# An expert's overflow products in two visits of TensorE, and their activations transposed by halves

## The reference

```python
logits = jnp.matmul(xt, w_router).astype(jnp.float32) + b_router.astype(jnp.float32)
top_logit, top_idx = lax.top_k(logits, TOP_K)            # TOP_K = 4, 32 experts
gates = jax.nn.softmax(top_logit, axis=-1)
...
gu = lax.ragged_dot(xs, w_gate_up, group_sizes) + b_gate_up[e_sorted]
gate, lin = jnp.split(gu, 2, axis=-1)
gate = jnp.minimum(gate, SWIGLU_LIMIT)                   # 7.0
lin = jnp.clip(lin, -SWIGLU_LIMIT, SWIGLU_LIMIT)
act = (lin + 1.0) * (gate * jax.nn.sigmoid(SWIGLU_ALPHA * gate))
out = lax.ragged_dot(act, w_down, group_sizes) + b_down[e_sorted]
```

## Time and profile before

| what | us |
|---|---|
| median of 3 runs | 2567.62 (2565.17 to 2568.31) |
| span of the profiled execution | 2566.9 |
| TensorE busy | 2471.5 (96%) |
| VectorE busy | 1506.3 (59%) |
| ScalarE busy | 1226.7 (48%) |
| GpSimd busy | 329.9 (13%) |

### The profile page before, as it was taken

How to read it: one execution, slowest core, us unless ns; L and a number is a source line. 1 busy time by engine, 2 the same in 40 slices (tenths; PEclk the granted TensorE clock), 3 DMA queues, 4 the chain that set the end, 5 groups by cost and what they waited for, 6 DMA issues and landing times.

```text
span 2566.9 us, 41888 instructions
## 1 busy us (share of the span) xinstructions
PE 2471.5 (96%) x14427; PEld 1980.3 (77%) x14428; DVE 1506.3 (59%) x1486; ACT 1226.7 (48%) x1246; POOL 329.9 (13%) x379
## 2 busy tenths in 40 slices
PE   8999999999999989976999999999999999999996
PEld 7987777998888878974788777777777886778775
DVE  4312333332333235355789876888876997688877
ACT  6413444220112021064577665666655775667665
POOL 0000000000000000042121212121121221212110
PEclk9999999999999999997999999999999999999998
DMA  4133243224332212447789987898977997899988
GB/s 129 34 50 54 66 73 80 49 50 49 50 50 81 99 66 91 146 167 263 257 317 384 371 296 257 319 381 287 369 252 258 376 381 271 306 335 331 387 278 304
DMA packets 262285, 536.68 MB, mean 209 GB/s; under 512 B 28952, under 2 KB 79896, under 8 KB 261120
## 3 DMA queue, kind: packets, MB, share of 16 engines
q1 hardware_dynamic: 241184, 488.96, 57.3%
q0 software_dynamic: 21024, 46.65, 6.7%
HBM read 492.92 MB, written 42.63 MB: 209 GB/s over the span
## 4 chain that ended last, share of the span: by engine, by line
PE 51%; DMA 1%; DVE 1%; issue 0%; ACT 0%; POOL 0%; ACTq 0%; POOLq 0%; DVEq 0%
PE m_y L2158 5%; PE m_gate L2158 5%; PE m_gate L2162 4%; PE m_lin L2158 4%; PE m_gate L2160 4%; PE m_lin L2162 4%; PE m_lin L2160 4%; PE m_y L2160 4%; PE m_y L2162 4%; PE m_spill L2200 4%; PE m_turn L2212 2%; PE m_turn L2150 1%; PE m_gate L2168 1%; PE m_y L2168 1%; PE m_spill L2196 1%; PE m_lin L2168 1%
## 5 line engine op out<-in xcount | busy, mean ns | idle before, releaser
L1973 DVE TENSOR_TENSOR m_w_lo<-raw,m_w_hi 128x2048 fp32r<-128x2048 f32 x384 | 874.6, 2288 | 253.7 <-ACT m_w_hi L1847 234.8
L1847 ACT CAST m_w_hi<-raw 128x2048 fp32r<-128x2048 f32 x384 | 733.3, 1911 | 446.2 <-PE m_lin L2162 230.1
L106 PE MATMUL c_bank<-h_hi_r,ring_hi 128*128 128x512 f32 x640 | 251.7, 393 | 0.9 <-PEq L396 0.9
L108 PE MATMUL c_bank<-h_lo_r,ring_hi 128*128 128x512 f32 x640 | 249.5, 390 | 0.0
L109 PE MATMUL c_bank<-h_hi_r,ring_raw_r 128*128 128x512 f32 x640 | 249.2, 389 | 0.0
L147 ACT CAST ring_hi<-ring_raw 128x2048 fp32r<-128x2048 f32 x43 | 82.1, 1908 | 280.4 <-DMA ring_raw<-in_w_in 128.3
L2158 PE MATMUL m_gate<-m_w_hi,m_x_hi 128*128 128x512 f32 x512 | 209.6, 409 | 0.0
L2158 PE MATMUL m_y<-m_w_hi,m_a_hi 128*128 128x512 f32 x512 | 206.1, 403 | 1.5 <-DVE m_a_lo L2025 1.5
L2162 PE MATMUL m_gate<-m_w_hi,m_x_lo 128*128 128x512 f32 x512 | 201.1, 393 | 0.0
L2160 PE MATMUL m_y<-m_w_lo,m_a_hi 128*128 128x512 f32 x512 | 201.0, 393 | 0.0
L2158 PE MATMUL m_lin<-m_w_hi,m_x_hi 128*128 128x512 f32 x512 | 200.7, 392 | 0.0
(11 more groups left out here) (336 smaller groups left out, 4539.9 us busy)
## 6 DMA issues: line engine op xcount, KB each, us to landing
raw<-in_w_gate_up SPq DMA_DIRECT2D x512, 512.0 KB
raw<-in_w_down SPq DMA_DIRECT2D x256, 512.0 KB, 12.3
ring_raw<-in_w_in SPq DMA_DIRECT2D x31, 1024.0 KB, 9.4
gates<-work POOLq DMA_DIRECT2D x32, 256.0 KB, 2.6
work<-gates SPq DMA_DIRECT2D x8, 1024.0 KB, 7.2
v<-in_x SPq DMA_DIRECT2D x8, 512.0 KB, 12.5
ring_raw<-in_w_branch_b SPq DMA_DIRECT2D x4, 1024.0 KB, 5.3
ring_raw<-in_w_branch_a SPq DMA_DIRECT2D x4, 1024.0 KB, 5.2
```

Of the source, the lines that this page charges most:

```text
L106: pe.matmul(out, left_hi(k), right_hi(k), start=first and k == kts[0], stop=False, skip_group_check=True)
L108: pe.matmul(out, left_hi(k), right_lo(k), start=False, stop=False, skip_group_check=True)
L1847: act.copy(w_hi[:, p % WS].rearrange("p k b n -> p (k b n)"), raw[:, raw_slot(m)].rearrange("p k b n -> p (k b n)")).then_inc(signals.whi, 1)
L1973: dve.tensor_tensor(w_lo[:, p % WS].rearrange("p k b n -> p (k b n)"), raw[:, raw_slot(m)].rearrange("p k b n -> p (k b n)"), f32(w_hi[:, ...
```

## The change

TensorE's overflow products move into two visits. Behind p 5 stand `s_down(8)`, `s_down(9)` and `s_gate_up(4)` to `(7)`; behind p 11 stand `s_down(10)`, `s_down(11)` and, for the next expert, `s_gate_up(0)` to `(3)`. Ahead of the loop all four `s_gate_up` stand behind panel 3. Since the down product of panels 8 and 9 needs only the first half of the activations, each half is transposed alone: `s_turn(0)` behind p 4, `s_turn(1)` ahead of the panel of p 10, both into `p_turn`, and copied by `as_copy` at steps 5 and 10. The sums share one bank now: `s_y` (down) and `s_h` (one half of gate and up at a time) are the two halves of `p_spill`, and the second half's bias matmul no longer sets `start`. `store` waits, with the overflow's rows, for the next expert's four gate-up products in that bank, and `pick_expert(0, ..)` moves from step 3 of VectorE to step 5.

```diff
+        s_y, s_h = p_spill[:, 0:256], p_spill[:, 256:512]
...
-            def as_copy(hb, nb):
+            def as_copy(j, hb, nb):
                 with act.If(hb > 0):
-                    act.wait_ge(signals.s_turned, nb + (OPEN + 1))
-                    act.copy(a_s[:, :, :].rearrange("p k c -> p (k c)"), p_gate[1][:, 0:256]).then_inc(signals.s_copied, 1)
+                    act.wait_ge(signals.s_turned, 2 * nb + (OPEN + j + 1))
+                    act.copy(a_s[:, 4 * j:4 * j + 4].rearrange("p k c -> p (k c)"), p_turn[:, 0:P]) \
+                        .then_inc(signals.s_copied, 1)
...
                     act.wait_ge(signals.s_dn, 4 * nb + (OPEN + 4))
-                    act.activation(ys_out[:, :], p_turn[:, 0:256], ACT.Copy,
+                    act.wait_ge(signals.s_gu, GU * nb + 4 * hb_next + (OPEN + GU))
+                    act.activation(ys_out[:, :], s_y, ACT.Copy,
...
+                    if p == 5:
+                        as_copy(0, hb, nb)
-                    if p == 9:
-                        as_copy(hb, nb)
+                    if p == 10:
+                        as_copy(1, hb, nb)
...
                     if p == 3 and not tail:
                         x_split(0, t + 1)
+                    if p == 5 and not tail:
                         dve.wait_ge(signals.panel_done, count(t, 0))
                         dve.wait_ge(signals.s_gu, GU * nb + 5 * hb + OPEN)
                         pick_expert(0, t + 1, signals.picked_gu)
...
-            def s_turn(nb):
-                pe.wait_ge(signals.s_activated, 2 * nb + (OPEN + 2))
-                for j in range(2):
-                    tr = pe.transpose(p_gate[1][:, j * P:(j + 1) * P], act_s[:, j], cst["ident"][:, :])
-                tr.then_inc(signals.s_turned, 1)
+            def s_turn(j, hb, nb):
+                with pe.If(hb > 0):
+                    pe.wait_ge(signals.s_activated, 2 * nb + (OPEN + j + 1))
+                    pe.transpose(p_turn[:, 0:P], act_s[:, j], cst["ident"][:, :]).then_inc(signals.s_turned, 1)
...
                     if p == 10:
                         pe.wait_ge(signals.alo, 2 * t + (OPEN + 2))
+                        s_turn(1, hb, nb)
...
-                    if 2 <= p <= 5:
+                    if p == 4:
+                        s_turn(0, hb, nb)
+                    if p == 5:
                         with pe.If(hb > 0):
-                            if p == 2:
-                                pe.wait_ge(signals.s_taken, 2 * nb + (OPEN + 1))
-                            s_gate_up(p + 2)
+                            pe.wait_ge(signals.s_copied, 2 * nb + (OPEN + 1))
+                            pe.wait_ge(signals.s_taken, 2 * nb + (OPEN + 1))
+                            pe.wait_ge(signals.s_stored, nb + OPEN)
+                            s_down(8)
+                            s_down(9)
+                            for panel in range(4, GU):
+                                s_gate_up(panel)
...
-                    if 8 <= p <= 11 and not tail:
-                        with pe.If(hb_next > 0):
-                            if p == 8:
-                                pe.wait_ge(signals.xs_copied, nb + hb + (OPEN + 1))
-                                pe.wait_ge(signals.s_taken, 2 * nb + 2 * hb + OPEN)
-                            s_gate_up(p - 8)
-                    if p == 10:
-                        with pe.If(hb > 0):
-                            pe.wait_ge(signals.s_copied, nb + (OPEN + 1))
-                            s_down(8)
-                            s_down(9)
                     if p == 11:
                         with pe.If(hb > 0):
+                            pe.wait_ge(signals.s_copied, 2 * nb + (OPEN + 2))
                             s_down(10)
                             s_down(11)
+                    if p == 11 and not tail:
+                        with pe.If(hb_next > 0):
+                            pe.wait_ge(signals.xs_copied, nb + hb + (OPEN + 1))
+                            pe.wait_ge(signals.s_taken, 2 * nb + 2 * hb + OPEN)
+                            pe.wait_ge(signals.s_stored, nb + OPEN)
+                            for panel in range(4):
+                                s_gate_up(panel)
```

More of the change, by code:

```diff
@@ L1863, in s_sigmoid @@
                     act.wait_ge(signals.s_activated, 2 * nb + (OPEN + j))
-                    act.activation(gate_s[:, :], p_spill[:, 256 * j:256 * j + P], ACT.Sigmoid, scale=ALPHA) \
+                    act.activation(gate_s[:, :], s_h[:, 0:P], ACT.Sigmoid, scale=ALPHA) \
                         .then_inc(signals.s_sig, 1)
@@ L1869, in a_split, with store @@
                 act.copy(a_hi[:, 4 * j:4 * j + 4].rearrange("p k c -> p (k c)"), p_turn[:, :]).then_inc(signals.ahi, 1)
-            def as_copy(hb, nb):
+            def as_copy(j, hb, nb):
                 with act.If(hb > 0):
-                    act.wait_ge(signals.s_turned, nb + (OPEN + 1))
-                    act.copy(a_s[:, :, :].rearrange("p k c -> p (k c)"), p_gate[1][:, 0:256]).then_inc(signals.s_copied, 1)
-            def store(t, hb, nb, at):
+                    act.wait_ge(signals.s_turned, 2 * nb + (OPEN + j + 1))
+                    act.copy(a_s[:, 4 * j:4 * j + 4].rearrange("p k c -> p (k c)"), p_turn[:, 0:P]) \
+                        .then_inc(signals.s_copied, 1)
+            def store(t, hb, nb, hb_next, at):
                 act.wait_ge(signals.scattered, t + (OPEN + 1))
@@ L1916, in body @@
             def body(t, tail=False):
-                hb, nb, _, _ = about(act, held, t)
+                hb, nb, hb_next, _ = about(act, held, t)
                 for p in range(MP):
@@ L1945, in body @@
                 else:
-                    store(t, hb, nb, count(t, MP - 1))
+                    store(t, hb, nb, hb_next, count(t, MP - 1))
             split(0, 6, 0)
@@ L2096, in last_rows @@
                     dve.wait_ge(old_spill, 16)
-                    dve.scalar_tensor_tensor(out=ys_out[:, :], in0=p_turn[:, 0:256], scalar=f32(slot_out[:, 1, 1:2]),
+                    dve.scalar_tensor_tensor(out=ys_out[:, :], in0=s_y, scalar=f32(slot_out[:, 1, 1:2]),
                                              in1=xs_g[:, :], op0=ALU.mult, op1=ALU.add).then_inc(s_summed, 1)
@@ L2189, in into @@
                 def into(g):
-                    out = p_spill[SPILL * g:SPILL * (g + 1), 256 * j:256 * j + 256]
-                    return out.rearrange("p (b n) -> p b n", b=2)
+                    return s_h[SPILL * g:SPILL * (g + 1), :].rearrange("p (b n) -> p b n", b=2)
                 if m % 4 == 0:
@@ L2195, in s_gate_up @@
                         right = f32(b_split[:, :]).rearrange("p (b j n) -> p b j n", b=2, j=2)
-                        pe.matmul(into(g), f32(pick[:, 0, 0:SPILL]), right[:, :, j, P * g:P * g + P], start=True,
+                        pe.matmul(into(g), f32(pick[:, 0, 0:SPILL]), right[:, :, j, P * g:P * g + P], start=j == 0,
                                   stop=False, skip_group_check=True)
@@ L2206, in s_down @@
                     for g in range(NG):
-                        pe.matmul(p_turn[SPILL * g:SPILL * (g + 1), 0:256], f32(pick[:, 1, 0:SPILL]),
+                        pe.matmul(s_y[SPILL * g:SPILL * (g + 1), :], f32(pick[:, 1, 0:SPILL]),
                                   f32(b_split[:, 256 * g:256 * g + 256]), start=True, stop=False,
@@ L2211, in s_down @@
                     for g in range(NG):
-                        mm = pe.matmul(p_turn[SPILL * g:SPILL * (g + 1), 0:256], a_s[:, 2 * (m - GU) + k],
+                        mm = pe.matmul(s_y[SPILL * g:SPILL * (g + 1), :], a_s[:, 2 * (m - GU) + k],
                                        raw[:, raw_slot(m), k, g // 2, 256 * (g % 2):256 * (g % 2) + 256], start=False,
@@ L2293, in _ @@
                     pe.sem_inc(signals.panel_done, 2)
-                with pe.If(first_second > 0):
-                    if m == 1:
-                        pe.wait_ge(signals.xs_copied, OPEN + 1)
-                    if m >= 1:
-                        s_gate_up(m - 1)
-                    if m == 3:
-                        s_gate_up(3)
+            with pe.If(first_second > 0):
+                pe.wait_ge(signals.xs_copied, OPEN + 1)
+                for m in range(4):
+                    s_gate_up(m)
             with pe.Fori(0, last) as t:
```

12 lines of the change are left out of this document (4 added, 8 removed).

## The result

The changed kernel takes 2631.21 us (median of 4 runs, 2629.54 to 2632.28), the kernel before 2566.84 beside it (4 runs, 2565.17 to 2568.31): a ratio of 1.0254, interval 1.0241 to 1.0266. It is slower by 64 us where 35 us were to be won. The range, 2527 to 2548, does not hold the time, and none of the rivals has it.

What follows compares the result with a forecast made beforehand. The prediction took TensorE to bound the expert loop. Visits -29.0, pause -4.1, transposes +1.3 and the part ahead of the loop -2.9 sum to -34.7 us, giving 2532.9 us, range 2527 to 2548.

Steps and rivals of the forecast that it cites:

- The range: Whole kernel time: 2528 to 2540 us for the forecast's own terms, 2527 to 2548 with rival A counted in.
- item 3 of "New waits": VectorE's comparison at p 5 waits for mid-visit, the p 9 split queued behind it but needed three panels later; priced at nothing.
- Item 5: VectorE's four split slots: filled during a visit, then kept at plain-pass pace plus small overflow operations; priced at nothing.
- Visits: Expert loop: 83 of 116 stops for 32-column matmuls between panels go, 0.35 us each, 29.0 us won.
- The pause: TensorE's wait before the gate bias, after 7 passes with only the next expert's overflow, goes: 7 x 0.59 = 4.1 us.
- Transposes by halves: Overflow passes: two separate transposes instead of two together cost 0.1 us more, 13 times, +1.3 us (bounds 0.5 and 3).
- Ahead of the loop: Panel 3 ends earlier with all visits behind it; first-pass wait shrinks from 2.3 to about 0.4; 2.9 us won.
- A plain pass: A pass of the expert loop without any overflow was to stay at 35.9 us.
- Items 1, 2 and 4 to 6 of "New waits": Expert loop: possible waits over activation copy (cover 0.5 us), m_a_lo (0.4), overflow-row store, split slots, loads; priced at nothing.
- rival B: Price lies in conditionals and code, not visits, or returns inside the long runs; only pauses and first pass won: 2562, chance 0.05.
- A: Feeders late at the thin covers behind p 5 and at p 10: 1 us in 13 passes, 13 us, 2546; chance 0.12.
- C: 32-column matmuls count as little work, so visits halve the clock: 1.7 us at 34 visits, 58 us, 2591; chance 0.05.

Runs made afterwards that it cites:

- e6_pick4: The changed kernel with VectorE's comparison of experts at the front of step 4 in every pass, not at step 5: 2525.44 us, 0.9848 of before.
- e3_fill: The changed kernel with 14 matmuls on an unused bank ahead of p 6 in passes without an overflow, keeping TensorE busy: 2596.01 us, 1.012 of before.
- e9_pick4_late: The changed kernel with the comparison at step 4, behind the activation, not at step 5: 2559.02 us, 0.9972 of before.
- e5_before_last_visit: The kernel before with only the next expert's four overflow gate-up products gathered in one visit behind p 11: 2551.67 us, 0.994 of before.
- both repaired kernels: The changed kernel with the comparison at step 3 without overflow and step 5 with one (2527.18 us), and with it at step 4 always (2525.44 us).
- e2_before_pick5: The kernel before with only the comparison moved from step 3 to step 5: 2666.44 us, 1.0393 of before.

## Why the prediction was wrong, point by point

**The step that failed is item 3 of "New waits", which priced the move of the comparison at nothing.** The runs show 102.2 us in its place, 5.7 for each of 18 passes. Item 3 said that VectorE's comparison "now waits at p 5 for the middle of the visit", "with the split for p 9 queued behind it", and found that this split is needed three panels later. It asked what the comparison holds up, and not who waits for the comparison itself; and it looked at it only in a pass that has the visit. The reader of it is TensorE, with the bias of p 6, the next panel. (The middle is also misplaced: the comparison is let go after 64 of 112 records, 3.5 us in at 0.055 each, and not after 96 of 144.) In the 18 passes of 31 that have no overflow there is no visit as a cover, and the program has one order for both kinds. The rows to see it by were there: VectorE's 33.45 us of work in a plain pass of 35.91 say that an operation put further down its list comes later by all that stands between. Item 5 weighed VectorE by its pace alone. The pace was kept, as the 33.53 us of the plain pass after show; the order of its work is what failed.

**How the loss adds up.** The loop of the changed kernel is 102.2 us longer than that of `e6_pick4`. `e3_fill` has the same lateness with TensorE busy, and is 70.5 us longer: 18 x 3.92, which is 3.66 of wait and the 0.25 around it, as in `e9_pick4_late`. The other 31.7 are the clock. Against before, the loop is 69.1 us longer: 102.2 less the 33.1 that the change wins in it. Ahead of it, from the first transposes of the inputs, 1.9 are won and in the tail 3.3, which leaves 63.9; the spans differ by 2630.6 - 2566.9 = 63.7.

**The terms of the sum** came out, each for itself:
- Visits. Forecast 0.35 each, 83 of them, 29.0. Measured 0.34, which makes 28.2. The Trainium skill (TensorEngine Tiling (Array Packing), Key Properties) has the array drained at a change of the tiling mode; the trace agrees in so far as the price went with the number of changes between 128 and 32 columns (26 of them, 8.8 us), at equal work. It doesn't tell the drain from the conditional that each visit stands in. No run here has such a visit without its conditional, so which of the two makes the price is open.
- The pause. All 7 went, as forecast (4.1). In `e5_before_last_visit`, where only the last visit grew, they went as well. What the sum left out is the jump behind hb passes, where the next bias starts 0.42 us after the last record and 0.31 before: 0.9 us over 8 passes.
- Transposes by halves. An hb pass has four visits fewer and is 46.11 before and 44.84 after in the mean: 46.11 - 4 x 0.34 = 44.75, and 0.09 is left, as much as the 0.11 at the jump. Forecast was 0.1 for the transposes alone; they can't be told from nothing here. (Before, they stand behind p 8, where the code and the row at 1870.60 in the earlier trace rows have them, and not behind p 7.)
- Ahead of the loop. Forecast 2.9, measured 3.6 by the traces and 2.3 by the medians.
- A plain pass. Forecast 35.9, measured 36.14 in the mean of both repaired kernels for 36.01 before, 1.4 us over 11 passes. No wait shows it, but its place does: the first two matmuls of p 10, before and then in `e6_pick4`:
```profile
1366.01 0.39 PE L2158 MATMUL m_y<-m_w_hi,m_a_hi 128*128 128x512 f32 x1
1366.23 0.39 PE L2160 MATMUL m_y<-m_w_lo,m_a_hi 128*128 128x512 f32 x1
```
```profile
1353.18 0.50 PE L2164 MATMUL m_y<-m_w_hi,m_a_hi 128*128 128x512 f32 x1
1353.52 0.40 PE L2166 MATMUL m_y<-m_w_lo,m_a_hi 128*128 128x512 f32 x1
```
The second starts 0.34 after the first in place of 0.22. Just there, between the panel's waits and the panel, the change has put the conditional of `s_turn(1)`, which a plain pass doesn't take. That it is the cause was not tried.
- Items 1, 2 and 4 to 6 of "New waits". In the loop no wait of TensorE for the copy, for `m_a_lo` or for a load appeared.
- The range. A visit at 0.38 wins 2.5 us more and one at 0.30 loses 4; the bounds were added the other way round. Rightly they give 2530 to 2541 in place of 2528 to 2540, which decides nothing here.
- A figure of the text, not of the sum, was wrong: the visit behind p 5 is not 144 records in 8.0 us but 112 in 6.2. The 144 records are an expert's own in both visits. The visit in the changed kernel, from its first record to the next panel's bias:
```profile
1573.20 0.64 PE L2212 MATMUL m_spill<-b_split,m_pick 128*32 128x256 f32 x8
1573.66 1.91 PE L2217 MATMUL m_spill<-raw,m_a_s 128*32 128x256 f32 x32
1575.38 0.61 PE L2201 MATMUL m_spill<-b_split,m_pick 128*32 128x256 f32 x8
1575.81 3.64 PE L2205 MATMUL m_spill<-raw,m_xs 128*32 128x256 f32 x64
1579.38 0.50 PE L2174 MATMUL m_gate<-b_split,m_pick 128*128 128x512 f32 x1
```
6.18 us for 112 records is 0.0552 each, the pace of the earlier trace rows kept over twice the length; rival B had nothing here.

With the comparison in place, the loop of `e6_pick4` is 33.1 us under before and the stretch ahead of it 1.3, 34.4 in all, where 34.7 were forecast. That they agree so closely is in part luck: the plain passes and the jump behind hb passes cost 2.3 us that the sum lacked. Its ratio, 0.9848, makes more than that of 2567.6 us, 39. Of the rest, 3.3 us lie in the tail, 50.1 us from the last p 0 to the end for 46.7. `e2_before_pick5`, whose tail is the same program as before's, has the short tail too, so this isn't the change's. Nor is it the clock: before has a stretch of 3.4 us at half clock there (at 2538.0), but so has `e3_fill` (at 2569.4), with a tail of 46.7, while `e5_before_last_visit` has a tail of 49.8 without such a stretch while TensorE still works. The chain that ended last, shown from its last store on, in the kernel before and then in `e2_before_pick5`:
```profile
2552.63 5.18 DMA out<-raw
```
```profile
2655.26 2.65 DMA out<-raw
```
In `e5_before_last_visit` this store takes 5.75 us. So 2.5 of the 3.3 us are the last store's; what lengthens it in some executions is open, as are the last 1 to 2 us.

**The rivals.** A was the right kind, a feeder come late, but for the copy and for `m_a_lo`, in the 13 overflow passes at 1 us each. It was another operand, in the 18 other passes, at 5.7 us each. B fell with the visits' price. C, the only one on the slower side, named the clock, but as a result of narrow matmuls. In the visit above the granted clock was 1.00, as the window shows:
```profile
1573.20:1579.38 6.18, 6.18 (x113) 3.54 (x113) 5.46 (x5) 1.90 (x1) 0.00 (x0) 1.00 0.15 47
```
The clock fell behind idleness and not in the visits. That is what the Trainium skill says (TensorE: Matmul & The Clock Gate, Part 1), and the trace agrees: 0.50 behind each of 18 waits of 3.66 us, and 1.00 throughout the loop in `e3_fill`, where matmuls fill the same time.

## What to carry to other kernels

When an operation is moved down an engine's list, ask first who reads its result and when that reader is due, and ask it in every kind of pass, above all in those in which the moved partner does not run: a conditional on one engine is no cover for an unconditional step on another. An engine that is busy 93% of a pass has little slack for order, even if its pace suffices: one step later cost nothing here, two steps later 5.7 us a pass. And a wait of TensorE is to be priced with the clock behind it, which here added half as much again as the idle time itself.

## What the hardware showed that was not expected

- Idle time of 3.66 us on TensorE was followed each time by a stretch at granted clock 0.50, of 3.4 us (14 times) or 6.8 (4 times); the price in time is 1.8 us per event (31.7 us for 18). Idle times of 1.46 us had none in 18 cases, one of 2.35 us had one in two of four executions.
- A wait costs 0.25 us beside its idle time without any change of the clock: 0.16 because the last matmul before it overlaps with no other, and 0.09 behind it. So it is with 1.46 us of idle time, and within 0.01 us behind the fill and the 0.4 us pauses of `e3_fill`.
- Going into a run of 32-column matmuls, in a conditional, and out again costs 0.34 us (runs of 8 against 24 records), and the records inside keep 0.055 us each up to 112 in a row.
- Conditionals that are not taken were not always free: 0.11 us more from the first to the second matmul of p 10 in a plain pass, 0.11 more at the loop's jump behind hb passes (0.2 in `e5_before_last_visit`). Each has such a conditional newly at its place; none was tried alone.
